# Moving the samples' decode step from the first pass to the second, between the scatters and the GELU squares on GpSimd

## The reference

```
h = x + W_out[ concat(mLSTM heads (4 x 128), chunk-MLP (4 x 128)) ]( rmsnorm(x) )
h = h + HierMoE(rmsnorm(h))      # 1 of 4 groups, then 2 of 8 SwiGLU experts
h = h + sigmoid(h @ W_pg) * rmsnorm(p @ W_ple);  final rmsnorm
```

```
qk    = silu(conv(conv_state, qk_pre))                  # width 4
m_new = max(lf + m, ig);  w = exp(ig - m_new);  d = exp(lf + m - m_new)
C_new = d * C + w * v k^T      # 128 x 128 per sample and head
n_new = d * n + w * k
h_a   = (C_new q) / max(|n_new q|, exp(-m_new));  h_a = rmsnorm(h_a) * sigmoid(o)
```

## Time and profile before

| | |
|---|---|
| runs before, us | 2406.79, 2413.01, 2410.16; median 2410.16 |
| profiled execution, us | 2407.17, span of its core 2405.6, mean granted clock 0.958 |
| busy share of the span | TensorE 92%, VectorE 62%, ScalarE 40%, GpSimd 19% |
| first pass | chunk 0 from about 80 us, the last chunk's head norm at 630 us |
| second pass | TensorE's `chunk_mlp` of tile 0 at 667.65, of tile 15 at 1085.63 us |
| one tile's `route_1` on VectorE | 787.15 to 792.54 us |
| GpSimd idle before L1680, steps 0 and 1 | 8.86 and 10.66 us |
| GpSimd's column product of 32 (L1109) | 0.36 us |

### The profile page before, as it was taken

One profiled execution on the slowest core, in us unless ns is written; L12 is line 12 of the kernel. 1 busy time (PEld: TensorE's weight loads), 2 busy tenths in 40 slices (PEclk: granted clock), 3 DMA queues, 4 the chain that ended last, 5 costly groups with the idle time before them and its releaser, 6 DMA issues. The chain is left out here.

```text
span 2405.6 us, 34278 instructions
## 1 busy us (share of the span) xinstructions
PE 2222.8 (92%) x10675; PEld 1811.3 (75%) x10676; DVE 1492.0 (62%) x2827; ACT 971.3 (40%) x1567; POOL 466.8 (19%) x617
## 2 busy tenths in 40 slices
PE   6999988999599999997498999999999999979998
PEld 5878877788478888886377777777777777747775
DVE  5777787777644455554554548496664666845554
ACT  4334333344322222221344437475554555723332
POOL 1121443221123232232110000000000000023332
PEclk9999988999799999998699999999999999989999
DMA  6102112112523232221777568597775778744331
GB/s 217 61 31 82 61 40 96 44 57 97 178 85 108 96 117 96 96 96 47 270 269 287 190 249 320 211 369 284 286 294 198 279 281 338 297 167 148 133 135 57
DMA packets 159157, 407.04 MB, mean 169 GB/s; under 512 B 18699, under 2 KB 22211, under 8 KB 158846
## 3 DMA queue, kind: packets, MB, share of 16 engines
q1 hardware_dynamic: 137350, 337.15, 38.8%
q0 software_dynamic: 14560, 43.11, 5.3%
q10 hardware_dynamic: 7200, 26.22, 2.7%
HBM read 330.10 MB, written 84.82 MB: 172 GB/s over the span
## 5 line engine op out<-in xcount | busy, mean ns | idle before, releaser
L1959 DVE TENSOR_TENSOR w_lo<-raw,w_hi 128x2048 fp32r<-128x2048 f32 x196 | 435.0, 2286 | 48.7 <-ACT w_hi L1895 48.7
L1895 ACT ACTIVATE w_hi<-raw 128x2048 fp32r<-128x2048 f32 x196 | 358.2, 1933 | 25.0 <-DMA raw<-in_w 25.0
L212 PE MATMUL bank<-w_hi,mix_x 128*128 128x512 f32 x816 | 339.4, 416 | 16.9 <-DMA first_s<-in_b_s 6.5
L213 PE MATMUL bank<-w_lo,mix_x 128*128 128x512 f32 x816 | 329.6, 404 | 0.0
L214 PE MATMUL bank<-w_hi,mix_x 128*128 128x512 f32 x816 | 329.6, 404 | 0.0
L1860 PE MATMUL bank<-w_hi,x_hi 128*128 128x512 f32 x784 | 310.9, 397 | 2.1 <-DVE x_lo L1951 2.1
L1861 PE MATMUL bank<-w_lo,x_hi 128*128 128x512 f32 x784 | 310.7, 396 | 0.0
L1862 PE MATMUL bank<-w_hi,x_lo 128*128 128x512 f32 x784 | 310.5, 396 | 0.0
L212 PEld LDWEIGHTS bank<-w_hi,mix_x 128*128 128x128 f32 x816 | 160.8, 197 | 51.4 <-DVE mix_x L849 7.1
L214 PEld LDWEIGHTS bank<-w_hi,mix_x 128*128 128x128 f32 x816 | 160.3, 196 | 36.0
L213 PEld LDWEIGHTS bank<-w_lo,mix_x 128*128 128x128 f32 x816 | 161.3, 198 | 32.0
(11 more groups left out here) (286 smaller groups left out, 3946.7 us busy)
## 6 DMA issues: line engine op xcount, KB each, us to landing
raw<-in_w SPq DMA_DIRECT2D x192, 1024.0 KB, 8.2
y_dram<-y_sb ACTq DMA_DIRECT2D x50, 512.0 KB
xT_dram<-mix_x SPq DMA_DIRECT2D x34, 512.0 KB, 3.4
mix_x<-xT_dram SPq DMA_DIRECT2D x34, 512.0 KB, 4.3
raw_all<-in_w_in SPq DMA_DIRECT2D x24, 512.0 KB, 5.7
x_sb<-in_x_prompt SPq DMA_DIRECT2D x16, 512.0 KB
xr_sb<-in_x_prompt SPq DMA_DIRECT2D x16, 512.0 KB
h_dram<-h_sb SPq DMA_DIRECT2D x16, 512.0 KB
```

What stands on the lines that cost most here:

```text
L212: pe.matmul(bank[:, :], x_hi[:, k, :], wh[:, k, :], start=(k == 0), stop=False)
L213: pe.matmul(bank[:, :], x_hi[:, k, :], wl[:, k, :], start=False, stop=False)
L1895: return act.activation(out, in_, ACT.Copy)
L1959: dve.tensor_tensor(w_lo[slot(j, m)][:, cols], raw[m][:, cols], w_hi[slot(j, m)][:, cols].bitcast(F32), ALU.subtract).then_inc(lo_ready, 1)
```

## The change

The samples' conv and SiLU stay in the first pass, behind the same steps; all else of their decode step moves to the second. ScalarE keeps a tanh behind step 2. SyncE keeps the store of q and k behind step 4, and the loads of the next weights behind step 13 no longer wait for the samples' heads. In the second pass the buffers lie in a tile `dec` of their own, C goes in eight pieces of four rows (512 elements per partition) instead of four of eight rows, and `tiles` takes two tables: `within`, a function that the engine runs inside step u, and `behind`, one behind it. GpSimd runs `sample_abs`, `sample_maxima`, `sample_state`, `sample_c(0)` to `sample_c(7)` within steps 0 to 10 and `sample_heads` within 13, each between the scatter and the squares; ScalarE has its three parts behind 0, 1 and 12; SyncE issues nine small loads and two of C before its tiles and the rest behind 2 to 13. `sample_heads` takes its gain from a load of its own. The samples' tile waits for their `h_a` before it is loaded.

```diff
-            with nc.allow_non_contiguous_dma(reason="a few numbers per sample and head"):
-                for c, src in enumerate((sg_dram[0], sg_dram[1], a["state_m"][0])):
-                    sp_.dma_start(G(c), spread(src.rearrange("b (h z) -> (b h) z", z=1))).then_inc(d_loaded, 16)
-            sp_.dma_start(d_v, s_dram[2].rearrange("b (w v) -> (b w) v", v=VI)).then_inc(d_loaded, 16)
-            sp_.dma_start(d_n4, a["state_n"][0].rearrange("b h (w v) -> (b h w) v", v=VI)).then_inc(d_loaded, 16)
-            sp_.dma_start(d_n, spread(a["state_n"][0].rearrange("b h d -> (b h) d"))).then_inc(d_loaded, 16)
...
         def keep_qk():
-            sp_.wait_ge(d_silu, 1)
...
+        def first_pieces():
+            sp_.wait_ge(c_kept, 32)
...
-        chunks(step, {4: keep_qk, 7: keep_state, 8: lambda: keep_rest(1), 9: lambda: keep_rest(2), 10: keep_heads,
-                      13: keep_samples, NT - 2: next_pieces})(sp_)
+        chunks(step, {4: keep_qk, 13: first_pieces, NT - 2: next_pieces})(sp_)
...
-        def sample_gates():
-            act.wait_ge(d_gate, 1)
-            act.activation(G(8), G(7), ACT.Exp, scale=-1.0).then_inc(d_act, 1)
...
-        chunks(step, {2: sample_gates, 4: sample_exps, 11: sample_squares})(act)
+        def sample_tanh():
+            act.wait_ge(c_conv, 1)
+            act.activation(d_th, d_x, ACT.Tanh, scale=0.5).then_inc(c_tanh, 1)
+
+        chunks(step, {2: sample_tanh})(act)
...
+        def sample_conv():
+            hold(pool, c_loaded, 16 * 8)
+            pool.tensor_tensor(d_cs, d_cs, d_cw[:, 0:CW - 1, :], ALU.mult).then_inc(c_steps, 1)
+            pool.tensor_tensor(d_x, d_x, d_cw[:, CW - 1, :], ALU.mult).then_inc(c_steps, 1)
+            hold(pool, c_steps, 2)
+            pool.tensor_tensor(d_x, d_x, d_cb, ALU.add).then_inc(c_steps, 1)
+            for j in range(CW - 1):
+                hold(pool, c_steps, 3 + j)
+                pool.tensor_tensor(d_x, d_x, d_cs[:, j, :], ALU.add).then_inc(c_steps if j < CW - 2 else c_conv, 1)
+
+        def sample_silu():
+            hold(pool, c_tanh, 1)
+            pool.tensor_scalar(d_th, d_th, 1.0, 0.5, ALU.add, ALU.mult).then_inc(c_steps, 1)
+            hold(pool, c_steps, CW + 2)
+            pool.tensor_tensor(d_x, d_x, d_th, ALU.mult).then_inc(c_silu, 1)
+
+        chunks(step, {1: sample_conv, 3: sample_silu})(pool)
+        rstd_heads(NT - 1)
...
+VC = VI // 8
+CHUNKS = VI // VC
+CPIECE = VC * P
+dec = s2("dec", [P, 32 + 6 * VI + 5 * P + 3 * CPIECE])
+G = lambda c, w=1: dec[:, c:c + w]
+d_v, d_n4, d_k4, d_num, d_row, d_wv = (dec[:, 32 + c * VI:32 + (c + 1) * VI] for c in range(6))
+d_n, d_q, d_k, d_prod, d_kw = (dec[:, 32 + 6 * VI + c * P:32 + 6 * VI + (c + 1) * P] for c in range(5))
+d_big = [dec[:, 32 + 6 * VI + 5 * P + c * CPIECE:32 + 6 * VI + 5 * P + (c + 1) * CPIECE] for c in range(3)]
+d_c = [x.rearrange("p (v d) -> p v d", d=P) for x in d_big[0:2]]
...
+def tiles(step, behind={}, within={}):
+
+
+    def loop(eng):
+        def run(u, r, r_next, r_last):
+            if u in within:
+                step(u, r, r_next, r_last, within[u])
+            else:
+                step(u, r, r_next, r_last)
+            if u in behind:
+                behind[u]()
+
+        run(0, P, P, P)
+        run(1, P, P, P)
+        done = 2
+        for u in sorted({*behind, *within, NT - 1}):
+            if u < 2:
+                continue
+            if u > done:
+                with eng.Fori(done, u) as t:
+                    step(t, P, P, P)
+            if u < NT - 1:
+                run(u, P, P, P)
+            done = u + 1
+        run(NT - 1, P, NS, P)
+        run(NT, NS, 0, P)
+    return loop
+
...
+                if r_next == NS:
+                    sp_.wait_ge(d_ha_kept, 16)
...
+        def load_samples():
+            with nc.allow_non_contiguous_dma(reason="a few numbers per sample and head"):
+                for c, src in enumerate((sg_dram[0], sg_dram[1], a["state_m"][0])):
+                    sp_.dma_start(G(c), spread(src.rearrange("b (h z) -> (b h) z", z=1))).then_inc(d_loaded, 16)
+            sp_.dma_start(d_v, s_dram[2].rearrange("b (w v) -> (b w) v", v=VI)).then_inc(d_loaded, 16)
+            sp_.dma_start(d_n4, a["state_n"][0].rearrange("b h (w v) -> (b h w) v", v=VI)).then_inc(d_loaded, 16)
+            sp_.dma_start(d_n, spread(a["state_n"][0].rearrange("b h d -> (b h) d"))).then_inc(d_loaded, 16)
+            for dst, w in ((d_q, 0), (d_k, 1)):
+                sp_.dma_start(dst, spread(s1_dram[w].rearrange("b (h d) -> (b h) d", h=H))).then_inc(d_loaded, 16)
+            sp_.dma_start(d_k4, s1_dram[1].rearrange("b (w v) -> (b w) v", v=VI)).then_inc(d_loaded, 16)
+            for c in range(2):
+                load_c(c)
+
+        def c_rows(x, c):
+            return x[0].rearrange("b h (w v) d -> (b h w) (v d)", w=VQ)[:, c * CPIECE:(c + 1) * CPIECE]
+
+        def load_c(c):
+            if c > 1:
+                sp_.wait_ge(d_c_kept, 16 * (c - 1))
+            sp_.dma_start(d_big[c % 2], c_rows(a["state_C"], c)).then_inc(d_c_loaded, 16)
+
+        def keep_c(c):
+            if 0 < c < CHUNKS - 1:
+                load_c(c + 1)
+            sp_.wait_ge(d_c_new, c + 1)
+            sp_.dma_start(c_rows(o["C_s"], c), d_big[c % 2]).then_inc(d_c_kept, 16)
+
+        def keep_state():
+            sp_.wait_ge(d_mt, 1)
+            sp_.wait_ge(d_state, 1)
+            sp_.dma_start(o["n_s"][0].rearrange("b h (w v) -> (b h w) v", v=VI), d_n4).then_inc(d_out, 16)
+            with nc.allow_non_contiguous_dma(reason="32 scalars, four times"):
+                sp_.dma_start(sm_dram.rearrange("t (w z) -> (t w) z", z=1), G(10)).then_inc(d_m_kept, 16)
+
+        def keep_m():
+            sp_.wait_ge(d_m_kept, 16)
+            with nc.allow_non_contiguous_dma(reason="32 scalars"):
+                sp_.dma_start(o["m_s"].rearrange("l b h -> (l b h)"), sm_dram[:, 0]).then_inc(d_out, 16)
+            keep_c(0)
+
...
+        def load_heads():
+            sp_.wait_ge(d_h_kept, 16)
+            sp_.wait_ge(d_c_kept, 16 * CHUNKS)
+            sp_.dma_start(d_h8, sh_dram).then_inc(d_tokens, 16)
+            sp_.dma_start(d_o8, s_dram[3]).then_inc(d_tokens, 16)
+            sp_.dma_start(d_g8, a["hnorm_g"][0, :].partition_broadcast(NS)).then_inc(d_tokens, 16)
...
+        tiles(step, {2: keep_state, 3: keep_m, 4: lambda: keep_c(1), 5: lambda: keep_c(2), 6: lambda: keep_c(3), 7: lambda: keep_c(4),
+                     8: lambda: keep_c(5), 9: lambda: keep_c(6), 10: keep_row, 11: load_heads, 13: keep_samples})(sp_)
+        sp_.wait_ge(d_out, 32)
...
+        tiles(step, {0: sample_gates, 1: sample_exps, 12: sample_squares})(act)
...
+        def sample_abs():
+            hold(pool, d_loaded, 16 * 9)
             do(TS(G(9), G(1), -1.0, None, ALU.mult))
-            do(TT(d_x, d_x, d_cb, ALU.add))
             settle()
             TS(G(7), G(1), G(9), None, ALU.max).then_inc(d_gate, 1)
...
         def sample_state():
-            hold(pool, d_act, 4)
-            hold(pool, d_qk, 48)
+            hold(pool, d_act, 3)
...
-            do(TS(d_o8, d_o8, 1.0, None, ALU.add))
+            do(TS(d_o8, d_o8, 1.0, 0.5, ALU.add, ALU.mult))
...
-        chunks(step, {1: sample_conv, 3: sample_silu, 5: sample_state, 6: lambda: sample_c(0), 7: lambda: sample_c(1),
-                      8: lambda: sample_c(2), 9: lambda: sample_c(3), 12: sample_heads})(pool)
+        chunks(step, {1: sample_conv, 3: sample_silu})(pool)
...
+        def step(u, r, r_next, r_last, sample=None):
             if past(u, 0):
                 rstd_h(u - 1, r_last)
             if past(u, 1):
                 scatter(u - 2, P)
+            if sample:
+                sample()
             if r_next:
                 gelu_squares(u + 1, r_next)
...
-        tiles(step)(pool)
+        tiles(step, within={0: sample_abs, 1: sample_maxima, 2: sample_state, 3: lambda: sample_c(0), 4: lambda: sample_c(1),
+                            5: lambda: sample_c(2), 6: lambda: sample_c(3), 7: lambda: sample_c(4), 8: lambda: sample_c(5),
+                            9: lambda: sample_c(6), 10: lambda: sample_c(7), 13: sample_heads})(pool)
```

More of the change, by code:

```diff
@@ L415, in step @@
                                     keep_ha(t - 1)
-                            def spread(src):
-                                return src.unsqueeze(1).to_broadcast([TB, VQ, src.shape[-1]])
-                            def quarters(c):
-                                return slice(c * PIECE, (c + 1) * PIECE)
                             def load_samples():
@@ L1316, in _, with spread @@
                                 sp_.dma_start(first_s[:, 1, :], a["b_s"][0, :, 0].partition_broadcast(NS)).then_inc(small_loaded, 16)
-                            tiles(step)(sp_)
+                            def spread(src):
+                                return src.unsqueeze(1).to_broadcast([TB, VQ, src.shape[-1]])
+                            def load_samples():
[10 more added lines that the diff above has]
```

(1 more changed line is left out.)

292 lines of the change are left out of this document (119 added, 173 removed).

## The result

The changed kernel takes 2414.8 us (median of 20 runs, 2411.3 to 2419.5); the kernel before took 2408.5 us beside it (20 runs). The ratio is 1.0024, 95% interval 1.0018 to 1.0031: slightly slower, by less than the 0.3% that the prediction counted as a difference (its case of 0.14). It had forecast 20 us less, and 2414.8 is above its range of 2377 to 2407. The profiled execution has a span of 2414.0 us against 2405.6. The 8.4 us between the two spans come from the starts of the chunks' and tiles' work in the two traces: -0.6 before the first pass's first chunk, -38.7 over its fifteen periods (526.4 to 487.8), +1.3 between the passes, **+45.1 over the second pass** (tile 0 to tile 15, 418.0 to 463.1) and +1.2 behind it. The forecast had -41.4 and +21.0.

The account below looks back on a forecast made before the run. TensorE was taken to bound the first pass, a chain through several engines the second. With 41.4 us less in the first and 21.0 more in the second, the profiled 2407.17 gave 2386.8; forecast 2390 us, range 2377 to 2407.

Parts of the forecast that it names:

- case of 0.14: The chance given to a time within 0.3%, 7.2 us, of the kernel before; faster had 0.80, slower 0.06.
- What leaves the first pass: First pass: moving the samples' work out of its steps saves 41.4 us, bounds 34 to 47.
- four quarter steps: First pass: four steps with a quarter of C on GpSimd, 162.86 us together, become plain ones of 32.5: 32.9 less.
- S: Second pass: GpSimd's time for one piece, an eighth of C, forecast at 9.6 us, between 9.2 and 10.
- DMAs and queues: Second pass: the moved loads and stores and ScalarE's sample work cost 0, at worst 2 us for the second tile's x.
- The loop through GpSimd: Second pass: from one first GELU product of VectorE to the next by scatter, piece and squares: 20.5 + S, 30.1 us.
- The period of the tiles: Second pass: a tile takes the longer of GpSimd's 30.1 us and the ring's 28.17, so +1.95 for most pieces.
- VectorE's ring: Second pass: the chain GELU product, norm, residual, h, hn, TensorE's projection, split of mix, routing, product again: 28.17 us a tile.
- Clock: Second pass: forecast counted 0 for half clock; the rival (0.12) had every lengthened tile pay 2.7 us or more, 2402.
- Hidden piece: Rival (0.10): with S under 8.0 us the pieces fit GpSimd's slack, about 4 us show in the second pass, 2373.
- Blocked routing: Rival (0.06): the piece's ladder holds up VectorE's routing in the second pass, 5 us a tile, 2419.
- The rule on S: Skill rule that GpSimd's one-input operations run near line rate: S at least 0.5 us shorter; forecast used the measured rows.

Follow-up runs that it names:

- run 11: The changed kernel with an Exp and a Ln, and so two table loads, put back on ScalarE in the first pass: 2421.6 us.
- run 1: The changed kernel with SyncE's sample transfers moved from behind h's store to ahead of its wait for h: 2399.5 us.
- early_dma: The kernel of run 1, the changed kernel with the samples' transfers issued ahead of SyncE's wait for h: 2399.5 us.
- run 7: early_dma with C in eleven pieces of 384 elements (the last of 256) in place of eight of 512: 2404.2 us.
- run 6: early_dma with GpSimd's wait for the scatter to land moved from behind the scatter to behind the piece: 2393.8 us.
- run 10: The kernel of run 6 with a wait of GpSimd for VectorE's mix put in front of the piece: 2395.8 us.
- run 8: early_dma without the product of C with q and the adding ladder; only the second pass is compared, tiles 28.3 to 28.9 us.
- run 12: early_dma with the sums of C times q moved from GpSimd's adding ladder to ScalarE, nothing left out: 2389.3 us.

## Why the prediction was wrong, by its own steps

**What leaves the first pass** held. Forecast -41.4, measured -38.7. The four quarter steps gave 162.86 - 130.5 = 32.4 for 32.9; the gates' step 5.8 for 5.1, and run 11 shows the table loads to be its cause; squares and heads 1.1 for 2.1; the other steps, 31.8 or 33.4 as the clock falls, came 3.1 us longer in this trace; the conv 2.5 for 1.3, though this one step is 37.4 in some of the runs above and 39.9 in others that have the same first pass. The waits for kw went from five to one, as said.

**S** held: 9.2 to 9.5 us and 0.47 of semaphores, for the forecast 9.6 and 0.15.

**"DMAs and queues ... 0" is the step that failed.** The loop through GpSimd was taken with the landing of the kernel before, "moves this by up to 0.9, mean 17.2". But the load and store in each tile, and the two tiny ones of n and m, were costed by how long SyncE needs to issue them and who waits for SyncE. The store's issue was itself put too low, 1.05 to 1.34 us for "at most the 0.43", but nobody waits for that. Their price is in the scatter that is issued beside them and waited for: 19.6 us more of landing in nine tiles, 15.3 us of the kernel's time (run 1). The sum should have asked of each moved transfer which other transfer of the new place is waited for. With the transfers out of the scatter's way the kernel takes 2399.5 (run 1), inside the range though 9.5 above the forecast; with them in it 2414.8, outside.

**The period of the tiles** was right in its terms and wrong in its form. GpSimd's loop without the longer landing is 30.05 us for the forecast 30.1. But "the tile takes the longer of the two" treats GpSimd's loop and VectorE's ring as if neither lengthened the other. In early_dma the routing, held up by the squares, puts 0.8 us a tile on top of GpSimd's loop; that the tiles at full clock come out at 30.20 to 30.43 is therefore in part luck. What was missing is 8.2 us (447.2 - 418.0 - 21.0): 6 in the eight tiles, and the heads, whose two tiles grew by 4.6 us for a forecast of 1.6; the sample state's tile took 2.2 for 3.25.

**Clock** ("I take the second: 0"). The wait for hn grew from 0.9 to 1.0 us only, so its premise fell; but the waits at the chunk-MLP, 1.0 to 1.9 us in early_dma, came with a granted clock of 0.94 or 0.95 in five of eight tiles, where every such tile of the kernel before has 1.00. The Trainium skill (TensorE: Matmul & The Clock Gate, Part 1: The HAM clock gate) says that activity is what releases the throttle; by that, idling speaks against such a change, and here the trace agrees. In run 7 it costs 1.6 us in six of eleven tiles, 0.9 on average, a third of the rival's 2.7 a tile.

**Hidden piece** was refused for the right reason, but its boundary was wrong: "Slack ... 8.0 us" is true of GpSimd alone. Run 7 fits a piece of 7.8 us in it and pays 2.5 us a tile.

**Blocked routing** (0.06, "VectorE has 2 us to spare before the squares are there"). In the changed kernel this held: in seven of eight tiles VectorE's product starts on GpSimd's squares. But as soon as GpSimd is relieved (runs 1, 6, 7, 10) it is the routing, held up by the squares, with the half clock, that keeps the tiles near 30.7. The rival had the right mechanism and the wrong partner: not the piece's ladder, the squares that the piece displaces. Run 7 splits the two by its rows, 1.6 and 0.9 us a tile. What draws the half clock stays open: releasing the mix (run 10) gained nothing, and shortening the piece (runs 8, 12) made both less together.

**The rule on S**: one-input operations at roughly line rate on GpSimd (the Trainium skill, GPSIMD Engine Reference, 4.1 Engine selection). The decay of C, a TENSOR_SCALAR of 512 whose scalar is a column of SBUF, takes 1.58 us, the TENSOR_TENSORs of 512 between 1.03 and 1.29. The trace disagrees there, and agrees for the squares' TENSOR_SCALAR of 1,024 with two constants, 1.04 us where the TENSOR_TENSOR of 1,024 takes 1.90. The rows of before were the right ones to go by.

## What to carry to other kernels

When work moves to another place, its transfers move too, and they are to be priced by what else is in flight there and who waits for it, not by their issue or their size: the three small ones of n and m cost about as much here as six loads and eight stores of 256 KB. Issue them where they have landed before the next transfer that is waited for; here that was an edit of a few lines in SyncE's order, worth 15 us. And the idle time of a helper engine is not slack where its instructions hold up those of the engine on the ring: fit the piece so that what follows it stays where it was, and try small, waiting instructions on another engine, as run 12 does.
